# Sums of squares of the q and k rows from rounded halves, one product block later, and the scan stage's short group moved to the end

## The reference, cut to what matters

```python
proj = h @ w_in                                   # layer 0: q, k, v, z
qkv = jax.nn.silu(short_conv(qkv, conv_w))        # width 4, along the tokens
q = l2norm(q.reshape(B, T, 8, 128)) * 128 ** -0.5 # x * rsqrt(sum(x*x over the 128 channels) + EPS)
k = l2norm(k.reshape(B, T, 8, 128))
...
r = jax.nn.sigmoid(einsum(xblk, w_r) + b_r)       # layer 1, both directions
i = jax.nn.sigmoid(einsum(xblk, w_i) + b_i)
log_a = -RG_C * r * softplus(-lam); a = exp(log_a)
b = sqrt(-expm1(2 * log_a)) * (i * xc)            # then a linear scan over the tokens
```

## Time and profile before

| | us |
|---|---|
| three runs | 4372.8, 4380.4, 4381.5; median 4380.4 |
| profiled execution | 4387.2 |
| its span, first to last instruction | 4385.3 |
| projection of layer 0 | about 240 to 1575 of the span |
| scan stage | about 3885 to 4165 of the span, with a tail of VectorE after it |

### The profile page before, as it was taken

How to read it: one execution, slowest core, us unless ns; L and a number is a source line. 1 busy time by engine, 2 the same in 40 slices (tenths; PEclk the granted TensorE clock), 3 DMA queues, 4 the chain that set the end, 5 groups by cost and what they waited for, 6 DMA issues and landing times. The chain is left out here.

```text
span 4385.3 us, 80392 instructions
## 1 busy us (share of the span) xinstructions
PE 4018.2 (92%) x30036; PEld 3363.5 (77%) x30036; DVE 2588.3 (59%) x3235; ACT 2139.5 (49%) x4198; POOL 2075.6 (47%) x1527
## 2 busy tenths in 40 slices
PE   7699999999999969999999999969998699978779
PEld 2378878888788858888888888857887588866667
DVE  3234544544544558888888888865654522248853
ACT  4255565655656645555555555541111511158822
POOL 2255565555566547777777777751110512100032
PEclk9899999999999979999999999989999699988889
DMA  6245555555455557777777777754443323255144
GB/s 255 90 122 160 156 154 156 155 154 158 142 160 152 159 181 207 208 207 208 208 207 210 209 206 207 207 190 163 177 188 119 89 110 138 109 219 198 69 146 137
DMA packets 777423, 733.23 MB, mean 167 GB/s; under 512 B 111904, under 2 KB 703264, under 8 KB 760416
## 3 DMA queue, kind: packets, MB, share of 16 engines
q1 hardware_dynamic: 684032, 681.48, 50.1%
q10 hardware_dynamic: 93056, 47.19, 3.6%
HBM read 483.12 MB, written 245.33 MB: 166 GB/s over the span
## 5 line engine op out<-in xcount | busy, mean ns | idle before, releaser
L627 PE MATMUL pj_bank<-h_hi,pj_whi 128*128 128x512 f32 (+1 forms) x1920 | 726.0, 378 | 14.5 <-POOL pj_first L613 14.5
L627 PE MATMUL pj_bank<-h_lo,pj_whi 128*128 128x512 f32 (+1 forms) x1920 | 707.7, 369 | 0.0
L1403 ACT ACTIVATE dc_R<-dc_psE 128x256 f16<-128x256 f32 x864 | 285.0, 381 | 417.7 <-PE dc_psE L1287 417.6
L994 DVE RECIPROCAL pj_acc<-pj_acc 128x2304 f32<-128x2304 f32 x16 | 232.9, 14553 | 378.4 <-ACT pj_acc L900 378.4
L627 PEld LDWEIGHTS pj_bank<-h_hi,pj_whi 128*128 128x128 f32 x1920 | 363.3, 189 | 81.4 <-POOL pj_first L613 14.7
L783 POOL TENSOR_TENSOR pj_BD<-pj_E,pj_gi 128x512 f32<-128x512 f32 x144 | 157.3, 1093 | 544.8 <-ACT pj_E L934 544.8
L627 PEld LDWEIGHTS pj_bank<-h_lo,pj_whi 128*128 128x128 f32 x1920 | 363.1, 189 | 65.9 <-issue 8.3
L931 ACT ACTIVATE pj_E<-pj_E,pj_gi 128x128 f32<-128x128 f32 x576 | 183.9, 392 | 465.7 <-DMA pj_gi<-scratch_gates 465.7
L1466 DVE TENSOR_TENSOR dc_Y<-dc_psY,dc_pick 128x256 f16<-128x256 f32 x864 | 324.7, 418 | 116.2 <-PE dc_psY L1272 110.9
L627 PE MATMUL pj_bank<-h_hi,pj_first 128*128 128x512 f32 (+1 forms) x960 | 353.7, 368 | 0.0
L627 PE MATMUL pj_bank<-h_hi,pj_wlo 128*128 128x512 f32 (+1 forms) x960 | 353.5, 368 | 0.0
(11 more groups left out here) (281 smaller groups left out, 10667.5 us busy)
## 6 DMA issues: line engine op xcount, KB each, us to landing
dc_dd<-scratch_decays SPq DMA_DIRECT2D x288, 256.0 KB, 5.3
dc_tm<-scratch_tm SPq DMA_DIRECT2D x288, 192.0 KB, 2.5
pj_E<-scratch_cgrow SPq DMA_DIRECT2D x288, 128.0 KB, 3.8
scratch_decays<-pj_E SPq DMA_DIRECT2D x144, 256.0 KB, 3.9
scratch_decays<-pj_BD SPq DMA_DIRECT2D x144, 256.0 KB, 3.8
dc_fm<-scratch_fm SPq DMA_DIRECT2D x288, 128.0 KB, 3.4
dc_egr<-scratch_egrow SPq DMA_DIRECT2D x288, 128.0 KB, 3.8
scratch_o<-dc_ob SPq DMA_DIRECT2D x288, 128.0 KB, 4.1
```

The lines of the kernel that those rows point to most:

```text
L627: i = pe.matmul(self.bank[blk][:, 0:n], l[b][:, k, :], r[:, k, at:at + n], start=(m == 0), stop=(m == 3 * KT - 1))
L994: dve.reciprocal(acc[:, 0:TOK], acc[:, 0:TOK]).then_inc(s["recip"], 1)
L1403: act.activation(all_cols(R[q][p], l, True), split4(quart(bE[p]), l), ACT.Copy).then_inc(eR[p], 1)
```

## The change

1. The sum of squares is taken from two rounded halves. ScalarE's square now writes `sq_hi` (float32r, in `acc`); VectorE has a new step in the z stage ahead of `normalise`: `square_low` multiplies the row by itself and subtracts `sq_hi`, which gives `sq_lo` (in the room of `tm`). TensorE multiplies both by the ones as float32r, two matrix products for each block in place of one in float32, and waits for `sq_lo` too.
2. These products stand one block later: the first three blocks of the sums after blk 4 of the z stage (before: after blk 3), the last two after blk 0 of the next stage (before: after blk 4).
3. ScalarE's roots go with them: the first three blocks in `beside(1)` after take 4 (before: `beside(0)`, ahead of decay 2), the last two in the next stage behind take blk 0 (before: in `beside(1)`).
4. In the scan stage the short group is filled and read last of the five, not third.

```diff
+    T["ones_r"] = nc.alloc_sbuf_tensor_at("ones_r", [P, P], F32R, offset=nc.sbuf_base - 4 * (1 + 12 * KT + P))
...
-        acc = sb("acc", [P, CONV])
+        acc, acc_r = raw_under(nc, ctx, "pj_acc", [P, CONV])
-        tm = sb("tm", [P, NCH, P])
+        tm, tm_r = raw_under(nc, ctx, "pj_tm", [P, NCH, P])
+        sq, sq_lo = (t[:].rearrange("p c t -> p (c t)") for t in (tm, tm_r))
+        sq_hi, ones_r = acc_r[:, 0:TOK], T["ones_r"][:]
...
                     if part == 0:
                         pe.wait_ge(s["square"], nth(h, j, "qk"))
+                        pe.wait_ge(s["sq_lo"], nth(h, j, "qk"))
...
-                        pe.matmul(aux[b % 3][:, 0:n], T["ones"][:], acc[:, at:at + n], start=True, stop=True
+                        pe.matmul(aux[b % 3][:, 0:n], ones_r, sq_hi[:, at:at + n], start=True, stop=False)
+                        pe.matmul(aux[b % 3][:, 0:n], ones_r, sq_lo[:, at:at + n], start=False, stop=True
                                   ).then_inc(s["aux"], 1)
...
+                        if j == Z0 + 1 and blk == 0:
+                            norms(h, Q, 1)
+                        if j == Z1 + 1 and blk == 0:
+                            norms(h, K, 1)
-                        if j == Z0:
-                            norms(h, Q, blk - 3)
-                        if j == Z1:
-                            norms(h, K, blk - 3)
+                        if j == Z0 and blk == 4:
+                            norms(h, Q, 0)
+                        if j == Z1 and blk == 4:
+                            norms(h, K, 0)
...
                 def beside(h, j, first, part):
-                    if j == Z0:
-                        root(h, Q, part)
-                    if j == Z1:
-                        root(h, K, part)
+                    if j == Z0 and part == 1:
+                        root(h, Q, 0)
+                    if j == Z1 and part == 1:
+                        root(h, K, 0)
...
                 def stage(h, j, first):
                     decay(h, j, 0)
                     take(h, j, 0, first)
+                    if j == Z0 + 1:
+                        root(h, Q, 1)
+                    if j == Z1 + 1:
+                        root(h, K, 1)
...
+                def square_low(h, j):
+                    n = nth(h, j, "qk")
+                    dve.wait_ge(s["silu"], nth(h, j, "qkv"))
+                    if h:
+                        dve.wait_ge(s["tm_out"], 16 * nth(h - 1, V1, "kv"))
+                    dve.tensor_tensor(sq, act_row[:], act_row[:], ALU.mult).then_inc(s["plain"], 1)
+                    dve.wait_ge(s["plain"], n)
+                    dve.wait_ge(s["square"], n)
+                    dve.tensor_tensor(sq_lo, sq, sq_hi.bitcast(F32), ALU.subtract).then_inc(s["sq_lo"], 1)
...
                     if KINDS[j] == "z":
+                        square_low(h, j - 1)
                         normalise(h, j - 1)
...
-    FILL = [WIDE[0:1], WIDE[1:2], [(0, 0), (1, 0)], WIDE[2:3], WIDE[3:4]]
+    FILL = [WIDE[0:1], WIDE[1:2], WIDE[2:3], WIDE[3:4], [(0, 0), (1, 0)]]
```

More of the change, by code:

```diff
@@ L672, in phase_project_gdn @@
         names = ("const", "conv0", "conv1", "conv2", "conv", "pads", "silu", "square", "aux", "aux_read", "recip", "norm",
-                 "fm_out", "tm_out", "z_out", "fm_turn", "sides", "mask", "d_abs", "d_exp", "d_scaled", "d_done")
+                 "fm_out", "tm_out", "z_out", "fm_turn", "sides", "mask", "ones", "plain", "sq_lo", "d_abs", "d_exp", "d_scaled", "d_done")
         s = {q: sem("pj_" + q) for q in names}
@@ L846, in stage @@
                             turn(h - 1, V1, "trV1", blk - 3)
-                        if j == Z0:
-                            norms(h, Q, blk - 3)
-                        if j == Z1:
-                            norms(h, K, blk - 3)
+                        if j == Z0 and blk == 4:
+                            norms(h, Q, 0)
+                        if j == Z1 and blk == 4:
+                            norms(h, K, 0)
                         if j == V1:
                             turn(h, V0, "trV0", blk - 3)
+                pe.wait_ge(s["ones"], 1)
                 sweep(stage)
@@ L890, in silu @@
                         act.wait_ge(s["silu"], nth(h, j, "qkv"))
-                        act.activation(acc[:, 0:TOK], act_row[:], ACT.Square).then_inc(s["square"], 1)
+                        act.activation(sq_hi, act_row[:], ACT.Square).then_inc(s["square"], 1)
                 def root(h, j, part):
@@ L985, in _ @@
                 dve.memset(epsq[:], EPS * HD)
+                dve.tensor_copy(ones_r, T["ones"][:]).then_inc(s["ones"], 1)
                 dve.wait_ge(s["sides"], 32)
```

## The result

| | before | after |
|---|---|---|
| median | 4380.9 | 4501.9 (4501.0 to 4509.6, four runs) |
| ratio | | 1.028, 95% interval 1.0268 to 1.0293 |
| span of the profiled execution | 4385.3 | 4507.8 |

A forecast was written before the change was run, and what follows sets the result against it. It took a chain through ScalarE, VectorE and SyncE's queue, beside TensorE, to bound the projection. Late roots +104 us and scan -23 made +81 on 4380.4, rounded to 4460; 8-in-10 range 4405 to 4500.

The forecast's parts named there:

- the late root, VectorE's side: Projection: last two roots wait behind z's store and take blk 0, so the reciprocal starts 6.7 us late a tile.
- a discount: Projection, q's row: 6.3 of the 6.7 us arrive at k's SiLU, as the store before was held by GpSimd.
- which hides both: Projection, z stage: VectorE's idle time covers both square_low instructions, 3.07 us each; without cover they would cost 6.1.
- both delays are worse: Rival, chance 0.12: 7.9 us a tile, or square_low holding up GpSimd's products and the next chunk; 4490 and above.
- TensorE's side: Projection sums: TensorE stands 6.0 us for bank 0, 0 to 0.3 for the low half; loses 2.5 a tile.
- one of my own signs of being wrong: Projection: the prediction called itself wrong if TensorE's wait for L900 (bank 0) was under 4 us.
- k's row at the end of V0: Projection: TensorE waits there for the normalised k row, so k's delay of 6.7 us a head reaches it.
- The table loads: Projection, ScalarE: one more table load a tile at 1.28 us, 20 in all, without the skill page's 1.38 drain.
- The scan: Scan stage: with the short group last, ScalarE's wait for TensorE goes; 23 us saved, between 10 and 30.

The follow-up runs named there:

- e4: The changed kernel with both parts of the root back at their old places in ScalarE's order, TensorE's sums staying one block later: 4350 us.
- e5: The changed kernel with the second part of the root (last two blocks) moved up, ahead of decay 0 and take blk 0 of the next stage: 4354 us.
- e11: The changed kernel with z's store cut in two, the first three quarters issued after take 3, ahead of decay 2: 4481 us.
- e12: The changed kernel with both instructions of square_low replaced by single-input ones, making the low half zero: 4471 us.
- e2: The kernel before with only the new places of sums and roots; float32 sums, no low half, old scan order: 4503 us.
- e3: The kernel before with only the sums from rounded halves, at the old places and with the old scan order: 4402 us.
- e1: The kernel before with only the scan stage's short group filled and read last: 4349 us, ratio 0.994.
- e8: e4 with the normalised row's store moved behind chunk 1's store and load in SyncE's queue, in stages K and V0: 4351 us.
- e9: e4 with one of GpSimd's three decay products left out (the strict mask), so values are changed: 4333 us.
- e10: e1 with one of GpSimd's three decay products left out (the strict mask), so values are changed: 4330 us.
- e7: The kernel before with the normalised row's store moved behind chunk 1's store and load in SyncE's queue: 4369 us, ratio 0.9999.

## Why the prediction was wrong

**The direction and the mechanism were right.** The forecast said that the moved roots make the reciprocal late, and that this lateness goes through nearly whole, while TensorE's saving is lost. e4 takes the roots back and 152 us with them; e5 takes back only the second part, and 148. Across after, e11, e12 and e4 (all with the new scan, the halves and late sums) the time moves with the reciprocal: 28.1, 27.1, 26.0 and 18.3 against 4502, 4481, 4471 and 4350. From the first to the last that is 152 us over 9.8, 15.5 us of time for each us (14.9 against their own groups), and there are 16 tiles. The line ends at e4: e5's reciprocal comes 1.1 us earlier still and nothing is gained.

**The step that failed is the size of "the late root, VectorE's side".** I had 6.7 us a tile (4.8 to 7.9) and, after a discount, 13.0 a head, 104 in all. Measured: 9.9 a tile by the mean (28.1 - 18.2), 18.5 a head and 148 in all. Two things were missing.
- *The low half beside GpSimd, 2.3 us a tile, put at nothing.* I wrote that VectorE is idle there, "which hides both", and looked only at VectorE and TensorE. The rival "both delays are worse", at 4490 and above, named the collision, gave it no price of its own, and has the measured time in it. On VectorE the pair takes 7.0 us in the mean where I had 6.1, so little of the loss is there; GpSimd's work beside it is held, and the chunk comes late whose load then holds decay 0, a wait that isn't in my path at all. By e2's mean the halves add 28.1 - 25.8 = 2.3; e12, with both instructions shorter, takes 2.1 of it back, and 22 to 31 us. The Trainium skill, "SBUF — State Buffer", section "SBUF: two separate sides", says that VectorE with two SBUF inputs and a GpSimd instruction that reads SBUF take a shared pair of ports by an exclusive lock for a whole instruction; 2.39 that becomes 4.59 and 2.56 that becomes 4.63 agree with it. So do the ends: the split's, at 824.85, is 2.25 after that of VectorE's first instruction, and that of VectorE's second, at 827.26, is 2.41 after the split's.
- *z's store and the chunks' loads, 0.9 us a tile.* e2, with the new places alone, has 25.8 - 18.2 = 7.6 where I had 6.7. I moved z's store 1.3 us earlier and kept its 7.6 us, read off one tile (the mean was 8.1), and kept the chunk's 4.0. In e2 the store took 9.5 in the mean; in the changed kernel the load shown took 6.0. e11, which spreads the store, gets 12 to 21 us back. That the transfers slow each other is the reading that fits; no run here takes one of them away.

**TensorE's side was mis-sized in both directions.** For bank 0 it stands 2.1 us, not 6.0 (34.3 over 16), since it arrives late itself: it waits for the low half 72.5 us where 0 to 5 in all were foreseen. Under 4 us at bank 0 was one of my own signs of being wrong, and rightly: e5 keeps that stop and loses next to nothing by it. Those stops were no terms of their own. TensorE follows the others here. What I left out on its side is the clock: its granted clock over the same 1335 us was 0.99 before and is 0.94 now. Behind the stop that ends at 827.37 it is at its lower level part of the time (0.61 in the mean from 828 to 832), and there products of 256 columns follow each other in 0.21 us, not in 0.12:

```profile
240.00:1575.00 1335.00, 1185.59 (x5706) 1000.14 (x5705) 643.57 (x174) 730.55 (x1262) 673.04 (x470) 0.94 0.48 138
...
828.00:832.00 4.00, 4.00 (x21) 3.87 (x20) 0.00 (x0) 3.71 (x7) 2.90 (x4) 0.61 0.07 25
```
```profile
829.24 0.41 PE L628 MATMUL pj_bank<-h_lo,pj_whi 128*128 128x256 f32 x1
829.45 0.41 PE L628 MATMUL pj_bank<-h_hi,pj_first 128*128 128x256 f32 x1
...
832.50 0.28 PE L628 MATMUL pj_bank<-h_hi,pj_first 128*128 128x256 f32 x1
832.62 0.28 PE L628 MATMUL pj_bank<-h_hi,pj_whi 128*128 128x256 f32 x1
```

How much of the 148 us this carries, no run here separates; in e4 and e5, without the loss, the clock over 240 to 1600 is 0.97, and 0.98 in the kernel before.

**k's row at the end of V0** stops TensorE in all eight heads, 56.6 us, as forecast. **The table loads:** the trace again shows the next instruction 0.02 us behind the load, and nothing of the drain that the Trainium skill, "ScalarE: Activation LUTs", section "What ACT_TABLE_LOAD costs", adds. **The scan:** -23 forecast, -26.4 measured.

**Do the parts add up?** As far as these runs can tell: e2 and e3 with the scan's gain make 128 + 27 - 27 = 128, and the change 121 to 130, depending on the runs of before it is set against. But e3's 27 arise at TensorE, which has its sums at the old places there, so they need not be the same 27 in the whole change.

**What stays open:** what bounds the projection once the reciprocal is in time. 29 us less of TensorE's work show nowhere (e4 against e1, e8, e9 against e10). But TensorE's stops before the sums are 31.8 us in e4 and 17.9 in e1, so part of the saving went into the wait for the low half, and no run has the cheaper sums without that wait. SyncE's wait for the row isn't it (e7, e8), and the chunks' round is so only in part (e9, e10). A third pair of chunk buffers would be the clean test; it wasn't run. Open too are the clock's part in the loss, and how the low half's share divides between the length of its two instructions and their meeting with GpSimd.

The best version is the smallest: e1, the scan's line alone, at 4349, below both kernels. e4 at 4350 is not distinguishable from it.

## What to carry to other kernels

When a step is moved one slot later on the busiest engine, follow the semaphore it feeds through every in-order queue: here a root was put behind a chunk's load and a take that waits for a transfer, and 9.9 us of lateness in each of 16 tiles came to 148 us, while the engine that was to be helped only stood longer. Cover is a matter of ports and transfers too: an engine that is idle hides an instruction only if what runs beside it on the other engine is not slowed by it. Read an engine that is 97% busy against who waits for whom: e4 cuts its work and gains nothing.

## What the runs showed of the hardware

A GpSimd product of 128x1024 from SBUF beside VectorE products with two SBUF inputs took 4.59 us, not 2.39, and VectorE's took 4.63, not 2.56: both lost about 2.1 to 2.2 us, so the price is paid on both sides. A transfer of 10 KB issued 1.7 us behind one of 1.1 MB landed after about 6 us, with a median of 4.0 over the whole stage.
